# Three normed attentions of a two-stack transformer, written out pair by pair, with the next pair's queries and keys prepared during a pair's softmax

## The chip, the cores and the metric

The kernel runs on one core of one Trainium2 chip, as one launch. The metric is the device time of that launch in microseconds. The core has TensorE (PE), VectorE (DVE), ScalarE (ACT), GpSimd (POOL, unused here) and the queue of SyncE (SP), which issues the loads of weights. The engines run side by side and wait for each other on semaphores.

## The reference

A sequence of 256 tokens with 1024 features, all in float32, goes through two stacks of layers.

- Two layers of the first stack: `h = h + mix(norm(h)) @ w_out`, a gated feed-forward part and a gated projection of a side input. The mix concatenates a differential attention ("da": 4 heads, each with two query and key parts of 64 features and values of 128), a state-space mixer and a gated linear attention.
- Four layers of the second stack: a modulated norm, an attention, a gated add, another modulated norm and a feed-forward part. The attentions are, in order, stick-breaking ("sb"), block attention ("moba", here plain causal attention, since 256 tokens are one block), sliding window of 128 with sinks ("swa": 16 query heads, 2 key and value heads), and "sb" again.

In da, moba and swa (the three normed kinds) queries and keys are normed per head and turned by rotary angles:

```python
q = apply_rope(rms_norm(q, gain_q), cos, sin)
k = apply_rope(rms_norm(k, gain_k), cos, sin)
p = softmax(mask(q @ k.T / 8))          # da: softmax 1 - lambda * softmax 2
y = p @ v                               # da: rms_norm(y, g_sub) * (1 - lambda_init)
out = concat(y) @ w_out
```

## The kernel before

Activations are kept transposed: features on the 128 partitions, 256 tokens along the free dimension. A product with a weight is made in three fp32r matmuls (high part by high part, low activation by high weight, high activation by low weight, `three()`, L597 to L599), so each weight tile of 128x1024 is loaded by SP into a slot of `wslot`, rounded to `w_hi` by ACT (L1144, 1 us), and its rest `w_lo` made by DVE (L1506 or L1512, 1.2 us), which also frees the slot for SP's next load. Loads are issued by SP in a fixed order; for an attention it is, for each i: query tile i+1, key tile i+1, value tile i+1, output tile i, each when its slot is free.

An attention works on one pair of 64-wide heads at a time (one 128-wide tile; da: the two parts of one head). da has 4 such pairs and runs in two layers, moba 8, swa 8 in two groups of four. All pairs of a group in swa share one key and value tile, so a key and value tile is new ("fresh") for pairs 0 and 4 alone; in the others it is new for every pair. For a pair the work is:

- PE: project queries, and keys when fresh (24 matmuls each into `bank` 0); project values (L724, two halves of 16 recorded matmuls, plain fp32, into `bank` 1); sum squares over a head (L731); turn (L767); scores (L681, L682, into `bank` 2 and 3); transpose the weights of the softmax (L700, back into `bank` 2 and 3); values (L713, L714, `bank` 3, in da `bank` 1); da: sum squares of y (L735); output projection (24 matmuls into `acc`, L597 to L599).
- ACT: square (L1198), inverse root by Ln and Exp (L1148, L1150), exponentials of the softmax (L1242, L1247), copies of the transposed weights to `pt`, of the values to `v_sb` and of y to `y_hi` (all L1144), and the roundings of weight tiles.
- DVE: norming (L1487), the products with cos (L1614) and sin (L1616) and their sum (L1618, makes `qk`), mask and row maximum (L1487, L1630 to L1637), scaling by the inverse sum (L1537 to L1543), and the low parts of weight tiles and of y.

The order within a step of the loop, `whole(i, prior)`, is for PE: project queries and keys of pair i; transpose the weights of pair i-1; first half of the values of i; square sums of i; (moba, swa) y of pair i-1; second half of the values; (da) y of i-1; turn i; (moba, swa) output of i-1; scores of i; (da) output of i-1. So the softmax of pair i runs on DVE and ACT while PE is at the next step's projections of queries and keys. After the last pair there is nothing left to project: PE waits for its softmax, transposes, forms y and projects it. The middle steps run in a loop of the program (`Fori`), the first and the last are written out (`segments`).

## Time and profile before

| | us |
|---|---|
| median of 3 runs | 2418.82 (2411.75 to 2422.43) |
| profiled execution | 2425.04 |
| its span in the trace | 2423.1 |
| mean granted clock of TensorE | 0.959 |

Busy time of PE is 2239.9 us, of PE's weight loads 2101.7, of DVE 1576.0, of ACT 1073.9. The attentions that the change touches lie at these times of the trace: da of layer 0 from 28 to 130 us, da of layer 1 from 530 to 622, moba from 1379 to 1528, swa from 1745 to 1878. A step is read here from the start of one pair's scores to the start of the next pair's. The granted clock is 1.00 for 2.4 GHz and 0.50 for 1.2 GHz; a value between says which part of the stretch ran at either.

### The profile page before, as it was taken

What the parts mean: (1) busy time and instruction counts of PE and PEld (TensorE: products, weight loads), DVE (VectorE), ACT (ScalarE), POOL (GpSimd) and SP (SyncE); (2) the same over time, 40 slices, a digit from 0 to 9 for tenths busy, and PEclk for the clock granted to TensorE, in tenths of its full rate; (3) what the DMA queues carried; (4) which work ended last, traced back from release to release, by engine and by line L of the source; (5) the groups of instructions that cost most, each with busy time, mean ns of one, the idle gap of its engine ahead of it and who ended that gap; (6) DMA issues with size and microseconds to landing.
All of it is one profiled execution on the core that took longest, in us unless ns stands there. A gap on an engine that the chain in (4) does not pass through costs nothing.

```text
span 2423.1 us, 45499 instructions
## 1 busy us (share of the span) xinstructions
PE 2239.9 (92%) x17460; PEld 2101.7 (87%) x17460; DVE 1576.0 (65%) x2623; ACT 1073.9 (44%) x1728; POOL 0.2 (0%) x4
## 2 busy tenths in 40 slices
PE   5889999898889999899899999899987999998998
PEld 4788899877888999798899888799865999898998
DVE  4576677735665787366787866688866555666554
ACT  3445444324454443255444444444445444555442
POOL 0000000000000000000000000000000000000000
PEclk8999999998999999899999999899988999998999
DMA  4355399843552998454599654499832466442664
GB/s 135 89 148 156 114 302 291 257 126 106 140 143 82 300 298 276 133 156 132 163 300 299 217 155 142 138 297 300 250 88 87 130 186 187 139 138 86 192 182 138
DMA packets 549140, 436.19 MB, mean 180 GB/s; under 512 B 27664, under 2 KB 475192, under 8 KB 548920
## 3 DMA queue, kind: packets, MB, share of 16 engines
q1 hardware_dynamic: 545680, 431.22, 58.5%
q10 hardware_dynamic: 3368, 3.71, 0.5%
q8 instruction: 62, 1.02, 0.2%
q14 instruction: 30, 0.25, 0.0%
HBM read 433.82 MB, written 1.05 MB: 179 GB/s over the span
## 4 chain that ended last, share of the span: by engine, by line
PE 80%; DVE 10%; ACT 4%; DMA 2%; DVEq 2%; issue 2%; ACTq 1%; SPq 0%
PE bank L597 13%; PE bank L599 13%; PE bank L598 13%; PE acc L597 7%; PE acc L598 7%; PE acc L599 7%; PE bank L724 5%; PE bank L1111 2%; PE bank L1019 2%; ACT w_hi L1144 1%; PE bank L607 1%; DVE head_work L1487 1%; DVE w_lo L1512 1%; PE bank L767 1%; PE bank L713 1%
## 5 line engine op out<-in xcount | busy, mean ns | idle before, releaser
L597 PE MATMUL bank<-h_hi,w_hi 128*128 128x256 f32 x3024 | 856.7, 283 | 17.2 <-DVE w_lo L1512 4.6
L599 PE MATMUL bank<-h_hi,w_lo 128*128 128x256 f32 x3024 | 845.2, 279 | 0.0
L598 PE MATMUL bank<-h_lo,w_hi 128*128 128x256 f32 x3024 | 845.2, 279 | 0.0
L1144 ACT ACTIVATE w_hi<-wslot 128x1024 fp32r<-128x1024 f32 x574 | 595.2, 1055 | 516.7 <-PE acc L599 285.1
L1512 DVE TENSOR_TENSOR w_lo<-wslot,w_hi 128x1024 fp32r<-128x1024 f32 x396 | 474.5, 1221 | 229.8 <-ACT w_hi L1144 229.3
L597 PEld LDWEIGHTS bank<-h_hi,w_hi 128*128 128x128 f32 x3024 | 571.3, 189 | 41.2 <-issue 10.8
L599 PEld LDWEIGHTS bank<-h_hi,w_lo 128*128 128x128 f32 x3024 | 574.5, 190 | 0.0
L598 PEld LDWEIGHTS bank<-h_lo,w_hi 128*128 128x128 f32 x3024 | 572.2, 189 | 0.1
L597 PE MATMUL acc<-mid_hi,w_hi 128*128 128x256 f32 x1120 | 317.4, 283 | 5.2 <-DVE mid_lo L1803 3.2
L599 PE MATMUL acc<-mid_hi,w_lo 128*128 128x256 f32 x1120 | 312.6, 279 | 0.0
L598 PE MATMUL acc<-mid_lo,w_hi 128*128 128x256 f32 x1120 | 312.6, 279 | 0.0
L1487 DVE SCALAR_TENSOR_TENSOR head_work<-wslot,c_act,head_work 128x512 f32<-128x512 f32 x288 | 216.4, 751 | 24.0
L597 PEld LDWEIGHTS acc<-mid_hi,w_hi 128*128 128x128 f32 x1120 | 210.5, 188 | 7.5 <-DVE mid_lo L1803 3.6
L599 PEld LDWEIGHTS acc<-mid_hi,w_lo 128*128 128x128 f32 x1120 | 212.4, 190 | 0.0
L598 PEld LDWEIGHTS acc<-mid_lo,w_hi 128*128 128x128 f32 x1120 | 211.1, 188 | 0.0
L1506 DVE TENSOR_TENSOR w_lo<-wslot,w_hi 128x1024 fp32r<-128x1024 f32 x114 | 136.2, 1220 | 46.8 <-ACT w_hi L1144 46.6
L597 PE MATMUL acc<-y_hi,w_hi 128*128 128x256 f32 x384 | 128.2, 334 | 21.9 <-DVE y_lo L1556 21.9
L724 PEld LDWEIGHTS bank<-wslot,hT 128*128 128x128 f32 x1088 | 128.8, 193 | 9.1 <-issue 9.1
L724 PE MATMUL bank<-wslot,hT 128*128 128x128 f32 x1088 | 135.7, 279 | 0.0
L598 PE MATMUL acc<-y_lo,w_hi 128*128 128x256 f32 x384 | 119.2, 310 | 0.0
L599 PE MATMUL acc<-y_hi,w_lo 128*128 128x256 f32 x384 | 118.5, 309 | 0.0
L597 PEld LDWEIGHTS acc<-y_hi,w_hi 128*128 128x128 f32 x384 | 85.6, 223 | 30.5 <-issue 29.4
(267 smaller groups left out, 2497.8 us busy)
## 6 DMA issues: line engine op xcount, KB each, us to landing
wslot<-in_ada_w_dram SPq DMA_DIRECT2D x192, 512.0 KB, 5.8
wslot<-in_ffn_w_gate_dram SPq DMA_DIRECT2D x88, 512.0 KB, 4.8
wslot<-in_ffn_w_up_dram SPq DMA_DIRECT2D x88, 512.0 KB, 5.4
wslot<-in_ffn_w_down_dram SPq DMA_DIRECT2D x88, 512.0 KB, 3.5
wslot<-in_w_in_dram SPq DMA_DIRECT2D x72, 512.0 KB, 4.2
wslot<-in_sb_w_in_dram SPq DMA_DIRECT2D x48, 512.0 KB, 4.9
wslot<-in_w_ffn_gate_dram SPq DMA_DIRECT2D x44, 512.0 KB, 4.8
wslot<-in_w_ffn_up_dram SPq DMA_DIRECT2D x44, 512.0 KB, 5.5
```

Source lines behind the costliest of these rows:

```text
L597: pe.matmul(dst, w_hi[:, w, cols], hi, start=start, stop=False, skip_group_check=True)
L598: pe.matmul(dst, w_hi[:, w, cols], lo, start=False, stop=False, skip_group_check=True)
L599: return pe.matmul(dst, w_lo[:, w, cols], hi, start=False, stop=stop, skip_group_check=True)
L607: mm = pe.matmul(B(3, m, m + 1), ada_rows[:, P * m:P * m + P], C("ones", 0, 1), start=True, stop=True)
L713: pe.matmul(bank[c, y_bank, 0:256], v_sb[:, 0, c], pt[:, hh, 0:256], start=True, stop=False)
L724: mm = pe.matmul(B(1, 256 + P * t, 384 + P * t), hT[:, k, P * t:P * t + P], wk(2, k), start=(k == 0), stop=(k == KT - 1))
L1019: mm = pe.matmul(B(0, 0, 256), C("ones"), sqT[:, k, :], start=(k == 0), stop=(k == KT - 1))
L1111: mm = pe.matmul(B(2 * b, 0, 256), wk(s, k), xT[:, k, :], start=(k == 0), stop=(k == KT - 1))
L1144: return act.activation(dst, src, ACT.Copy)
L1487: return dve.scalar_tensor_tensor(out=out, in0=x, scalar=scalar, in1=y, op0=op0, op1=op1)
L1506: dve.tensor_tensor(w_lo[:, part, :], wslot[:, n, :], w_hi[:, part, :], ALU.subtract)\
L1512: dve.tensor_tensor(w_lo[:, part, :], wslot[:, n, :], w_hi[:, part, :], ALU.subtract).then_inc(slot_used[n], 1)
```

## The change

The function `attention` of each engine becomes two: `stick` for sb, which issues what it issued before (one wait that was long met is left out on PE), and `ahead` for da, moba and swa, which is written out for every pair, with no loop. SP's order is as it was. PE's order becomes:

```python
project(0); norm_sums(0); project_v(0); turn(0)
for i in range(n):
    more = i + 1 < n
    scores(i)
    if i and att == "da": out_sums(i - 1)
    if more: project(i + 1)
    whole = not more or fresh(i + 1)
    if i: out(i - 1, range(KT) if whole else range(4))
    if more:
        norm_sums(i + 1)
        if fresh(i + 1): project_v(i + 1)
    if i and not whole: out(i - 1, range(4, KT))
    if more: turn(i + 1)
    turn_weights(i)          # the transposes, L700 before
    values(i)
if att == "da": out_sums(n - 1)
out(n - 1, range(KT), att != "da")
```

ACT's order:

```python
square(0); root(0); v_copy(0); qk_high(1)
for i in range(n):
    if i and att == "da": y_root(i - 1)
    exps(i)
    if i and att == "da": y_high(i - 1)
    if more: square(i + 1)
    if i + 2 < n: qk_high(i + 2)          # else, not in da: two roundings for the feed-forward part
    if more: root(i + 1)
    if i: act.wait_ge(unit_done[3], g("unit_done3") + i)
    mix_high(3, PART_DOWN, unit_loads(at, att, 3, i))
    if more and fresh(i + 1): v_copy(i + 1)
    for hh in range(heads): ...           # copies of the transposed weights to pt
    act.wait_ge(sem["pv_done"], g("pv_done") + i + 1)
    ...                                   # da: square of y; else: y_hi
```

DVE's order:

```python
qk_normed(0); qk_turned(0); qk_low(1)
for i in range(n):
    maxima(i)
    if i and att == "da": y_normed(i - 1); y_low(i - 1)
    end_softmax(i)
    if i + 2 < n: qk_low(i + 2)           # else, not in da: two low parts for the feed-forward part
    if more: qk_normed(i + 1); qk_turned(i + 1)
    mix_low(3, PART_DOWN, i)
    if att != "da": y_low(i)
```

The tiles move in PSUM: square sums of queries and keys go from `bank` 2 to `bank` 1; values from `bank` 1 to columns 384 to 512 of `bank` 2 and 3; y of moba and swa from `bank` 3 to `bank` 1; the square sums of da's y to the second half of `bank` 1. `v_sb` is used in two halves in turn. New waits on PE: `project_v(i)` waits for the row maxima of pair i-1 (for pair 0 for a step of the modulation units that is older), the scores of pair 0 and the transposes ahead of a fresh pair wait for the copy of the values.

```diff
-                def whole(i, prior, kv, fresh, new_kv, more):
-                    ...
-                    proj_qk(i, ki, fresh, prior is None)
-                    if prior is not None:
-                        middle(prior)
-                    ...
-                    scores(i)
-                    if att == "da" and prior is not None:
-                        out(prior)
+                def project_v(i):
+
+                    loads = 32 if att == "swa" else 16
+                    pe.wait_ge(slot_full[2], 16 * (g("slot2") + g("extra2")) + loads * (group(i) + 1))
+                    pe.wait_ge(sem["h_ready"], g("h_ready"))
+                    if i:
+                        pe.wait_ge(sem["negmax"], g("negmax") + 2 * i)
+                    elif g("ada_stored"):
+                        pe.wait_ge(sem["ada_stored"], g("ada_stored") - 1)
+                    for t in range(TT):
+                        for k in range(KT):
+                            mm = pe.matmul(B(2 + t, 384, 512), hT[:, k, P * t:P * t + P], wk(2, k), start=(k == 0), stop=(k == KT - 1))
+                    mm.then_inc(slot_used[2], 1)
+                def values(i):
+                    width = P // heads
+                    v = P * (group(i) % 2)
+                    pe.wait_ge(sem["v_copied"], g("v_copied") + group(i) + 1)
+                    pe.wait_ge(sem["pt_ready"], g("pt_ready") + heads * i + heads)
+                    for hh in range(heads):
+                        c, d = slice(width * hh, width * hh + width), slice(v + width * hh, v + width * hh + width)
+                        pe.matmul(bank[c, 1, 0:256], v_sb[:, 0, d], pt[:, hh, 0:256], start=True, stop=False)
+                        mm = pe.matmul(bank[c, 1, 128:256], v_sb[:, 1, d], pt[:, hh, 256:384], start=False, stop=True)
+                    mm.then_inc(sem["pv_done"], 1)
```

## Rows read from the trace of the kernel before

**Rows 1.** The page's first part: busy us, share of the span, instructions, by engine.

```profile
PE 2239.9 (92%) x17460; PEld 2101.7 (87%) x17460; DVE 1576.0 (65%) x2623; ACT 1073.9 (44%) x1728; POOL 0.2 (0%) x4
```

**Rows 2.** Windows from scores to scores: length, busy by engine, clock, DMA share, GB/s.

```profile
53.65:69.83 16.18, 13.80 (x101) 11.68 (x102) 10.49 (x23) 6.97 (x18) 0.00 (x0) 1.00 0.49 142
69.83:91.61 21.78, 17.89 (x126) 16.00 (x126) 11.47 (x25) 9.08 (x21) 0.00 (x0) 0.92 0.34 98
...
113.49:130.30 16.81, 11.66 (x64) 10.29 (x65) 8.23 (x20) 6.57 (x16) 0.00 (x0) 0.80 0.50 125
...
560.31:583.05 22.74, 18.85 (x126) 16.96 (x126) 11.47 (x25) 9.09 (x21) 0.00 (x0) 0.85 0.33 95
...
1395.85:1415.05 19.20, 19.20 (x130) 16.88 (x130) 11.47 (x24) 8.15 (x18) 0.00 (x0) 0.83 0.53 143
1431.26:1447.48 16.22, 16.22 (x132) 14.22 (x131) 10.41 (x23) 8.17 (x18) 0.00 (x0) 1.00 0.41 127
...
1512.36:1528.17 15.81, 9.30 (x49) 7.72 (x48) 7.46 (x17) 7.46 (x15) 0.00 (x0) 0.69 0.24 71
...
1804.47:1820.74 16.27, 16.27 (x131) 14.21 (x130) 10.03 (x25) 7.58 (x19) 0.00 (x0) 1.00 0.22 65
...
1834.76:1848.71 13.95, 11.24 (x75) 8.56 (x75) 8.50 (x22) 6.73 (x18) 0.00 (x0) 0.88 0.25 75
...
1862.75:1878.19 15.44, 8.43 (x50) 6.97 (x49) 7.29 (x19) 7.95 (x17) 0.00 (x0) 0.67 0.24 68
```

**Rows 3.** PE's timeline, one middle step of moba: start, duration, what.

```profile
1431.26 0.50 PE L681 MATMUL bank<-head_work 64*128 64x128 f32 x4
...
1437.69 0.82 PE L700 MATMUL bank<-const,pr 128*128 128x128 f32 x6
1438.34 1.95 PE L724 MATMUL bank<-wslot,hT 128*128 128x128 f32 x16
1440.13 1.02 PE L731 MATMUL bank<-head_work,const 128*128 128x512 f32 x2
...
1441.89 2.05 PE L724 MATMUL bank<-wslot,hT 128*128 128x128 f32 x16
1443.78 1.02 PE L767 MATMUL bank<-head_work,const 128*128 128x512 f32 x2
```

**Rows 4.** PE's timeline in a middle step of swa, scores at 1820.74.

```profile
1827.03 1.00 PE L700 MATMUL bank<-const,pr 128*128 128x128 f32 x6 [2.42 <-DVE pr L1543]
1828.23 0.69 PE L731 MATMUL bank<-head_work,const 128*128 128x256 f32 x2 [0.20 <-ACT pt L1144]
```

**Rows 5.** DVE's timeline in the same step of swa.

```profile
1821.70 0.56 DVE L1487 SCALAR_TENSOR_TENSOR sm<-bank,const 128x384 f32<-128x384 f32 x1 [0.92 <-PE bank L682]
...
1827.09 0.35 DVE L1543 TENSOR_SCALAR pr<-pr,rinv 128x256 f32<-128x256 f32 x1
1827.35 1.22 DVE L1506 TENSOR_TENSOR w_lo<-wslot,w_hi 128x1024 fp32r<-128x1024 f32 x1
```

**Rows 6.** ACT's timeline in the same step of swa.

```profile
1825.72 0.19 ACT L1247 ACTIVATION_READ_ACCUMULATOR pr<-sm,nmx 128x1 f32 x1
...
1827.61 0.95 ACT L1144 ACTIVATE pt<-bank 128x384 f32<-128x384 f32 x2 [0.50 <-PE bank L700]
1828.96 0.47 ACT L1148 ACTIVATE head_work<-bank,epst 128x256 f32<-128x256 f32 x1 [0.40 <-PE bank L731]
```

**Rows 7.** PE's timeline, last step of da in layer 0, whose scores start at 113.49.

```profile
120.41 0.55 PE L700 MATMUL bank<-const,pr 128*128 128x128 f32 x3 [0.92 <-DVE pr L1487]
...
121.58 0.67 PE L713 MATMUL bank<-pt,v_sb 128*128 128x256 f32 x2 [0.63 <-issue]
...
123.04 0.67 PE L735 MATMUL bank<-ysq,const 128*128 128x256 f32 x2 [0.56 <-ACT ysq L1213]
```

**Rows 8.** Landing of the loads into wslot (L441) in moba, 1415 to 1465 us.

```profile
DMA to landing us min/median/max: 3.6/4.2/5.0
```

**Rows 9.** Landing of swa's half-tile loads of keys and values (L459).

```profile
DMA to landing us min/median/max: 4.7/5.4/8.2
```

More of the change, by code:

```diff
@@ L780, in attention, with whole @@
-                for lo, hi, *seg in segments(att, ph["n"]):
-                    if hi - lo == 1:
-                        whole(lo, lo - 1 if lo else None, *seg)
-                    else:
-                        with pe.Fori(0, hi - lo) as j:
-                            whole(j + lo, j + (lo - 1), *seg)
-                last = n - 1
-                middle(last)
-                values(last, 1 if att == "swa" else last)
+                def whole(i, prior):
+                    project(i, prior is None)
+                    if prior is not None:
+                        later_sums(prior)
+                        pe.wait_ge(sem["v_copied"], g("v_copied") + i)
+                    project_v(i, 0)
+                    if prior is not None:
+                        values(prior)
+                    project_v(i, 1)
+                    if prior is not None:
+                        out(prior)
+                    scores(i)
@@ L1256, in attention @@
[L1256 to L1262 removed]
+                    mix_high(3, PART_DOWN, unit_loads(at, "sb", 3, i))
+                    if not more:
+                        high(0, 2, unit_loads(at, "sb", 0, n))
@@ new lines, in ahead, with qk_low @@
+                mix_low = lambda m, part, i: low_of(m, part, g(f"high{m}") + i + 1)
+                heads = 1 if att == "da" else 2
+                group, fresh = grouping(att, n)
+                gains = qk_gains(att, l)
+                cos, sin = (cos1[:, :], sin1[:, :]) if att == "da" else (C("cos2"), C("sin2"))
+                mask = C("window") if att == "swa" else C("causal")
+                def qk_low(i):
+                    mix_low(0, 0, i)
+                    if fresh(i):
+                        mix_low(1, 1, group(i))
@@ L1612, in whole, with qk_normed @@
+                def qk_normed(i):
+                    sides = 2 if fresh(i) else 1
+                    dve.wait_ge(sem["qk_rs"], g("qk_rs") + i + 1)
+                    for side in range(sides):
+                        c = slice(256 * side, 256 * side + 256)
+                        last = stt(qkn[:, c], bank[:, 0, c], gains[side], rs2[:, c])
+                    last.then_inc(sem["qk_n"], 1)
                     dve.drain()
                     each = lambda ap: ap.rearrange("p (a s) -> p a s", a=sides)
-                    dve.tensor_tensor(each(qkc[:, 0:width]), each(qkn[:, 0:width]), per_tile(cos, sides), ALU.mult)
+                    dve.tensor_tensor(each(qkc[:, 0:256 * sides]), each(qkn[:, 0:256 * sides]), per_tile(cos, sides), ALU.mult)
@@ L1615, in whole, with qk_turned @@
+                def qk_turned(i):
+                    sides = 2 if fresh(i) else 1
+                    width = 256 * sides
+                    each = lambda ap: ap.rearrange("p (a s) -> p a s", a=sides)
                     dve.wait_ge(sem["qk_rot"], g("qk_rot") + i + 1)
```

548 lines of the change are left out of this document (296 added, 252 removed).

## The prediction

> **What bounds the kernel now.** I read the page first: PE is busy for 2239.9 us of the span, 92% [rows 1], so time can come only from PE's idle stretches, from stretches at the lower clock, and from what PE is given to do. PE's work is not changed in amount. I then cut the attentions into windows from one pair's scores to the next pair's [rows 2]. Three pictures come out. A middle step of moba takes 16.22 us, PE is busy for all of it and the clock is 1.00: nothing can be won there. A middle step of da takes 21.78 us with PE busy for 17.9 at a clock of 0.92; the four such steps are 21.78, 21.88, 22.74 and 21.91 long. A step of swa whose next pair shares keys and values takes about 14 us (six of them, the row shown is 13.95, the longest 14.50) with PE busy for 11.2 at 0.88. Last I took the timelines of single steps for the order and the price of each piece [rows 3 to 7].
>
> **Prices of the pieces**, start to start at full clock [rows 3]: scores 0.86; a fresh projection of queries and keys 5.57 (1432.12 to 1437.69), of queries alone half, 2.78; six transposes 0.65; each half of the values' projection 1.79; square sums 0.95; turn 0.95; values' product 0.80; an output projection 2.75 (from 1443.78 plus the turn to the next scores at 1447.48). They add up to 16.2 for a fresh step. With one-sided sums and turn (0.5 each) and no values a swa step is 8.8, a fresh da step with its three transposes and one more square sum is about 16.3.
>
> **The chain beside PE**, counted from the start of the scores at 1820.74 [rows 4 to 6]: mask at +0.96, exponentials done at +5.2, scaled weights done at +6.7, first transpose at +6.3. From the square sums' matmul to Ln 0.73; Ln and Exp take 0.97 for one side, 1.3 for two. From the turn to the next scores it is 2.57 for two sides (1.06 to the product with sin, then three DVE steps).
>
> **The stall that the new order brings.** Transposes and the product that reads their copy now stand next to each other on PE. In the trace there lies other work between them. ACT's two copies start 0.58 after the first transpose and take 0.95 [rows 4, 6], so the product starts 1.6 after it, where PE was free after 0.65: 0.95 idle in each pair of moba and swa. For da it is one copy; the last step of layer 0 shows the pair next to each other already, from 120.41 to 121.58 = 1.17, of which PE idles 0.84 at full clock. The bounds are 0.6 (the idle stretch that the row itself gives) [rows 7] and 1.3. Queued behind the product on PE is the next pair's scores and so its whole softmax, so this is paid in full.
>
> **A middle step of moba.** Scores 0.86, projection to 6.43, output to 9.18, sums to 10.1, values' projection to 13.7, turn to 14.7, transposes, stall to 16.3, product to 17.1. The norm (root ends at 11.6, normed at 12.5) is in time, `qk` is ready at 13.7 + 2.6 = 16.3. So 17.1 against 16.22: 0.9 slower, six times: **+5.4**. The first step (19.20 before at a clock of 0.83) loses the output projection (2.75), which goes to the end, and gains the stall and 0.8 of waiting for the square: **-1.1**. In the last step (15.81, PE idle 6.5) the output of pair 6 fills part of the wait for the softmax. Transposes start at 5.8 as before; ACT has one rounding ahead of the copies and not two, so the output starts about 1 us sooner; with the clock still low: **-1.5**. Moba: **+2.8**.
>
> **A middle step of da.** 0.86 + 0.5 + 5.57 + 2.75 + 0.95 + 3.6 + 0.95 + 0.33 = 15.5, stall 0.84, product 0.76: 17.05. y of the pair before is normed on DVE after the maxima (+3.9), rounded by ACT after the exponentials (+4.9), its low part done at 5.8; PE wants it at 7.0. PE's waits of before, 3.9 us in all (21.78 less 17.89), for the root of y ahead of the scores and then for `y_lo`, are gone, and with them the drop of the clock. Against 21.78, 21.88, 22.74, 21.91 that is 4.7 + 4.8 + 5.7 + 4.9 = **-20.1**. The first steps: -1.6 in layer 0 (16.18 before) and 0 in layer 1. The head of layer 0 is **+1.8**: half of the values' projection was done while ACT was still making the rotary tables, and now all of it stands behind the sums. The last steps get worse: the output of pair 2 waits for `y_lo` until 5.8 with nothing to cover it, where it started right behind the scores; PE idles for 4.4, so it runs at half clock (5.1), and transposes start at 10.9 where they started at 6.9 (120.41 less 113.49). **+3.5** in each layer, bounds +1.7 (clock up) and +4. Da: -20.1 - 1.6 + 1.8 + 7 = **-12.9**.
>
> **A step of swa within a group.** PE is free of its projection at 3.6 and of four output tiles at 5.0; ACT's square waits for the exponentials (5.1), sums at 5.5 to 6.1, second half of the output to 7.4. ACT rounds q(i+2) (5.4 to 6.4), then the root, to 7.3. DVE ends the softmax at 6.7, makes the low part of q(i+2) (1.22) [rows 5], and norms at 7.8 to 8.2: PE turns at 8.3 after a wait of 0.85. Transposes 8.8, product 10.4, end 11.2. So **11.2**, idle 0.5 + 0.85 + 0.95, against about 14: 2.8 less. Steps 1 to 2, 4 to 5 and 5 to 6 give -3.3, -2.8, -2.75. Step 0 to 1 starts at the lower clock: -1.4. In step 2 to 3 the keys of the second group are wanted one step earlier, and their half tiles land late, 4.7 to 8.2 after issue, with slow issues [rows 9]: +3, so +0.1 in all. Step 3 to 4 is a fresh one: 17.1 against 16.27, +0.8. Step 6 to 7 carries two roundings for the feed-forward part: -1.6. The last, 15.44 before, -1.8. Swa: **-12.75**.
>
> **Costs taken as nothing.** Without the loops: two turns of moba's loop both take 16.22 with PE busy throughout [rows 2], so a turn costs nothing now. The heads of layer 1's da, moba and swa: square sums come sooner, but the values' projection (da) and DVE's work on the modulation units (moba, swa) set the turn as before. The earlier roundings: SP now issues output tile i and queries i+2 at the very start of step i, since the slot of output i-1 is freed only after the norming. At 3.6 to 5.0 to land [rows 8] queries are there at about 4.5 to 5.4, ACT wants them at 5.4 in swa and at 7.1 or later elsewhere; keys two issues later.
>
> The Trainium skill, in "Runtime: NRT & Kernel Launch", section "Instruction fetch mechanics", says that a taken branch can force a fetch of instructions by DMA and advises unrolling. If each of the nine loop turns that go had cost one landing of rows 8 (4.2), the kernel would gain 38 us more, by an estimate; the two equal turns of moba speak against it.
>
> **Sum.** +2.8 - 12.9 - 12.75 = **-22.9**. Against the profiled execution, 2425.04, that is 2402.1; the median of the runs shown is 6.2 lower, 2418.82, which gives **2396**.
>
> **Rivals.**
>
> 1. The clock falls in swa in spite of shorter stalls. For: 2.3 us of 11.2 are idle, in three pieces. Against: up to 123.04 in the last step of da PE idled in three pieces, 0.92, 0.63 and 0.56, and the sums at 123.04 still took 0.67, what the values' matmuls took before them [rows 7]; the falls in swa follow one idle stretch of 2.42 [rows 4]. Price: a step at 0.88 has a quarter of 13.95 at half clock, 1.7 us of lost work [rows 2]; six steps: +10. Total -13, **2406**. The Trainium skill, "TensorE: Matmul & The Clock Gate", section "A second HAM failure mode: psum-queue depth-cycling", tells of a kernel whose short pauses between groups of matmuls made the clock swing; by it this rival would be the forecast. Chance 0.15.
> 2. The copies overlap better than I think, or a gap is hidden. Without the copy stall (19 pairs, 17 us) it is -40: **2379**. Rows 7 show the stall, so 0.08.
> 3. On the other side: weights come late. SP's in-order queue holds queries i+2 behind output tile i, which waits for the end of DVE's step. ACT's rounding stands ahead of the root, the root ahead of turn, transposes and the next scores: each us beyond the slack is a us in 16 steps. The point is a landing 4.9 after issue in swa and about 9.5 in fresh steps. At 2.2 us past it in each, +35: **+12, 2431**. Against: 5.0 is the longest whole-tile landing [rows 8], and 41% of the DMA engines are in use in moba [rows 2]. Chance 0.12.
> 4. The gains of da and swa are mostly eaten by waits between engines that I have not placed (five in-order hand-overs in a swa step, each taken at 0.05 to 0.1): -10 to 0, **2413**. Chance 0.15.
>
> My forecast has 0.50. What a measurement of this kernel tells from no change is about 0.5%, 12.1 us. The forecast and rival 2 are beyond it, and half of rival 1: 0.66 faster. Half of rival 1 and rival 4: 0.22 the same. Rival 3: 0.12 slower. The range goes from near rival 2, 2378, to 2418, past rival 4 and short of rival 3.
>
> **What would show it.** Right: middle steps of da near 17.0 with a clock of 1.00, steps of swa near 11.2, of moba near 17.1 with an idle stretch of 0.95 ahead of the values' product released by ACT's copies; the last step of da longer than before, with PE waiting over 4 us for `y_lo`. Wrong: moba's steps still 16.2 (no copy stall); swa at 13 or more with a clock under 0.95 (rival 1); ACT idle on a load into slot 0, 1 or 3 (rival 3).

## The result

The changed kernel takes **2392.3 us** (median of 7 runs, 2383.0 to 2396.5) against 2417.3 for the kernel before on the same chip (2409.4 to 2422.4): ratio 0.9894, 95% interval 0.9876 to 0.9911. The forecast was 2396. In a later comparison on another occasion the same kernel gave 2393.5 and 0.9899 (0.9867 to 0.9931).

The profiled execution has a span of 2390.4 us. Its engine line answers to [rows 1]: PE is busy 24.0 us less, with the same 17460 instructions. Of this 12.6 lie in the three attentions, where the granted clock is higher (over swa 0.90, and 0.87 before); the other 11.4 lie in the other stages, in several of which one and the same matmul took 281 ns in the first profile and 276 in this one (more on this at the second profile of the kernel before, among the experiments).

```profile
PE 2215.9 (93%) x17460; PEld 2083.6 (87%) x17460; DVE 1579.9 (66%) x2623; ACT 1076.5 (45%) x1728; POOL 0.2 (0%) x4
```

The windows of the changed kernel, from one pair's scores to the next pair's, answer to [rows 2] (length, then busy time by engine, granted clock, DMA share, GB/s):

```profile
54.70:69.62 14.92, 13.36 (x99) 11.38 (x100) 11.86 (x24) 7.50 (x16) 0.00 (x0) 1.00 0.49 145
69.62:86.47 16.85, 16.18 (x127) 14.40 (x126) 11.45 (x25) 9.35 (x20) 0.00 (x0) 1.00 0.44 126
...
585.73:607.39 21.66, 13.12 (x69) 11.47 (x68) 9.08 (x21) 7.55 (x19) 0.00 (x0) 0.76 0.82 201
1373.97:1391.16 17.19, 15.47 (x107) 12.97 (x107) 11.99 (x23) 7.87 (x17) 0.00 (x0) 0.90 0.65 177
1408.24:1425.33 17.09, 16.36 (x133) 14.57 (x131) 10.65 (x23) 8.37 (x18) 0.00 (x0) 1.00 0.45 123
...
1743.21:1755.98 12.77, 9.16 (x50) 6.80 (x50) 9.14 (x22) 6.27 (x17) 0.00 (x0) 0.77 0.15 42
1768.05:1782.69 14.64, 10.14 (x76) 8.41 (x75) 9.74 (x23) 7.72 (x19) 0.00 (x0) 0.92 0.63 144
1782.69:1801.61 18.92, 18.20 (x132) 16.08 (x130) 9.42 (x23) 7.80 (x19) 0.00 (x0) 0.88 0.18 57
1801.61:1813.05 11.44, 9.51 (x76) 8.17 (x74) 8.96 (x23) 6.71 (x18) 0.00 (x0) 1.00 0.33 92
```

A middle step of da takes 16.85 at a clock of 1.00, where it took 21.78 at 0.92. Moba's is 17.09, with PE busy for all but 0.73, against 16.22. A swa step within a group takes 11.44 to 12.07, the last one before the end of swa 13.44. Besides moba's, two kinds of window are worse than before: da's last step (21.66, clock 0.76) and the fourth step of swa (18.92, clock 0.88), with the late-key step ahead of it (14.64).

To see where the 32.7 us between the two spans went, I divided both traces at the matmuls of the norm on either side of each attention; in da the far mark is the first matmul of the mixer's small projection. The last two columns are a second profile of each kernel, taken with the experiments below.

| stretch | before | changed | difference | second profiles |
|---|---|---|---|---|
| da, layer 0 | 109.7 | 105.6 | -4.1 | 111.3, 105.9 |
| da, layer 1 | 101.8 | 94.0 | -7.8 | 104.1, 92.9 |
| moba | 160.6 | 162.4 | +1.8 | 157.8, 161.2 |
| swa | 144.1 | 136.8 | -7.3 | 145.5, 139.1 |
| the four | 516.1 | 498.8 | -17.4 | 518.7, 499.1 |
| all the rest | 1907.0 | 1891.6 | -15.4 | 1898.2, 1893.6 |

So the attentions give 17 to 20 us by both pairs of profiles. The rest of the difference lies in the other stages. Their only edit is the wait left out of the stick-breaking attention, whose middle steps take 15.65 to 15.84 before and after.

In a middle step of moba PE's timeline shows the new order, and its one gap (start, duration, what, in brackets the idle time before it and what ended it), answering to [rows 3]:

```profile
1422.12 1.02 PE L771 MATMUL bank<-head_work,const 128*128 128x512 f32 x2
1422.98 0.82 PE L791 MATMUL bank<-const,pr 128*128 128x128 f32 x6
1424.52 0.66 PE L801 MATMUL bank<-pt,v_sb 128*64 128x256 f32 x4 [0.72 <-ACT pt L1196]
1424.97 0.42 PE L802 MATMUL bank<-pt,v_sb 128*64 128x128 f32 x4
1425.33 0.50 PE L780 MATMUL bank<-head_work 64*128 64x128 f32 x4
```

Turn, transposes, the bare copy (0.72), values' product, scores: as forecast, with a gap of 0.72 in place of 0.95.

In swa the late keys show as the longest wait of PE. These are its timeline around the fourth pair's turn, and the turns of the sixth and the seventh pair, which have no new keys behind them:

```profile
1779.13 0.70 PE L771 MATMUL bank<-head_work,const 128*128 128x256 f32 x2 [3.51 <-DVE head_work L1583]
1779.66 0.82 PE L791 MATMUL bank<-const,pr 128*128 128x128 f32 x6
1781.21 1.13 PE L801 MATMUL bank<-pt,v_sb 128*64 128x256 f32 x4 [0.72 <-ACT pt L1196]
...
1810.17 0.70 PE L771 MATMUL bank<-head_work,const 128*128 128x256 f32 x2 [0.96 <-DVE head_work L1583]
...
1822.07 0.70 PE L771 MATMUL bank<-head_work,const 128*128 128x256 f32 x2 [1.45 <-DVE head_work L1583]
```

The wait of 3.51 is followed by half clock: the product at 1781.21 takes 1.13, not 0.66. DVE's norm is named as the releaser of all three turns, but ACT's timeline ahead of the last of them shows what was late, and DVE's how it reaches the norm:

```profile
1819.31 1.06 ACT L1196 ACTIVATE w_hi<-wslot 128x1024 fp32r<-128x1024 f32 x1 [0.81 <-DMA wslot<-in_swa_w_in_dram]
1820.27 0.46 ACT L1200 ACTIVATE head_work<-bank,epst 128x256 f32<-128x256 f32 x1
1820.80 0.42 ACT L1202 ACTIVATE head_work<-head_work 128x256 f32<-128x256 f32 x1
```

```profile
1820.40 1.22 DVE L1602 TENSOR_TENSOR w_lo<-wslot,w_hi 128x1024 fp32r<-128x1024 f32 x1 [0.64 <-ACT w_hi L1196]
1821.54 0.48 DVE L1583 SCALAR_TENSOR_TENSOR head_work<-bank,pcol,head_work 128x256 f32<-128x256 f32 x1
```

The rounding of the weights of the pair after next waits for their landing. Two things that the norm needs stand behind it: the root in ACT's order, done at 1821.22, and the low part of the same weights in DVE's order, done at about 1821.6. The second ends last here, by some 0.3 to 0.4.

### The profile page after: what moved, and what is told of

Read it like the earlier page. It is cut to its first block, busy times and chain, and to the rows that moved or that the text cites. A ratio compares the mean times of both kernels' runs of the same rounds, so it can differ in the third digit from the quotient of the medians.

```text
span 2390.4 us, 45059 instructions
## 1 busy us (share of the span) xinstructions
PE 2215.9 (93%) x17460; PEld 2083.6 (87%) x17460; DVE 1579.9 (66%) x2623; ACT 1076.5 (45%) x1728; POOL 0.2 (0%) x4
## 4 chain that ended last, share of the span: by engine, by line
PE 79%; DVE 9%; ACT 5%; DMA 4%; DVEq 1%; issue 1%; ACTq 1%; SPq 0%
PE bank L604 13%; PE bank L606 13%; PE bank L605 13%; PE acc L604 7%; PE acc L606 6%; PE acc L605 6%; PE bank L707 3%; PE bank L1163 2%; PE bank L1071 2%; PE bank L760 2%; ACT w_hi L1196 2%; DVE w_lo L1608 1%; PE bank L614 1%; DVE head_work L1583 1%; DMA wslot<-in_swa_w_in_dram 1%
## 5 line engine op out<-in xcount | busy, mean ns | idle before, releaser
L604 PEld LDWEIGHTS bank<-h_hi,w_hi 128*128 128x128 f32 x3024 | 571.1, 189 | 40.8 <-issue 11.1
L1602 DVE TENSOR_TENSOR w_lo<-wslot,w_hi 128x1024 fp32r<-128x1024 f32 x114 | 136.8, 1221 | 77.2 <-ACT w_hi L1196 77.0
L604 PE MATMUL acc<-y_hi,w_hi 128*128 128x256 f32 x384 | 121.4, 316 | 18.5 <-DVE y_lo L1745 15.8
L1552 ACT ACTIVATE silu_g<-bank 128x256 f32<-128x256 f32 x132 | 49.5, 375 | 115.8 <-PE bank L606 115.4
L2133 DVE TENSOR_TENSOR mid<-silu_g,bank 128x256 f32<-128x256 f32 x132 | 55.1, 417 | 61.3 <-ACT silu_g L1552 61.1
```

The costliest lines, as they stand in the source:

```text
L604: pe.matmul(dst, w_hi[:, w, cols], hi, start=start, stop=False, skip_group_check=True)
L1552: act.activation(silu_g[:, b, :], B(b, 0, 256), ACT.Silu).then_inc(sem["silu_ready"], 1)
L1602: dve.tensor_tensor(w_lo[:, part, :], wslot[:, n, :], w_hi[:, part, :], ALU.subtract)\
L2133: dve.tensor_tensor(mid[:, b, :], silu_g[:, b, :], B(b, 256, 512), ALU.mult).then_inc(sem["mid"], 1)
```

## The experiments

Each stretch below is measured between the same marks as in the table. The times of whole kernels scatter by some 10 us from run to run, so where 1 to 5 us are in question the steps of the profile decide.

**Moba alone in the old order.** The old function is kept beside the new one and called for moba:

```
-                    (stick if ph["att"] == "sb" else ahead)(ph, at)
+                    (stick if ph["att"] == "sb" else attention_old if ph["att"] in ('moba',) else ahead)(ph, at)
```

> The changed kernel with the moba attention alone as it was before the change (its three-part order, its loop over the middle pairs, values' bank as it was); da and swa as changed. Theory: the changed order costs moba 0.87 us a pair, 0.72 of it the bare copy behind the transposes, so here the steps of moba go back to 16.2 (first 19.2) from 17.09 (first 17.19), the stretch between the norms on its two sides from 162.4 to about 160.6, and the time is about 2 us below that of the changed kernel (ratio to before near 0.989). Rival: the longer step comes from something that reaches the whole kernel (the longer straight instruction stream, other addresses); then the steps stay near 17.1 and nothing is won. In both cases the steps of da stay at 16.85 and those of swa at 11.4 to 18.9.

Measured: 2396.5 us, ratio 0.9916 (0.9892 to 0.9941). The middle steps of moba are back at 16.20 to 16.23 (the first step is 17.79, not the 19.2 expected); its stretch is 158.6. Da's middle steps stay at 16.86 and 17.15. So the longer step comes with the new order, as the theory says, but not all of the 0.87 is the order's own price. Moba's middle steps in the new order take 16.79 or 17.09 in the nine profiles that have it as it stands in the changed kernel (38 steps and 16), and the 0.30 between the two is the level of the same matmul, 276 or 281 ns, as set out at the second profile of the kernel before. The 24 middle steps in the old order, in four profiles, all ran at the faster level. At equal level the order costs 0.57 a step. In the whole time it does not show: the interval holds the changed kernel's ratio too.

**Transposes early in da and moba**, so that the copy is covered:

```
                     whole = not more or fresh(i + 1)
+                    if early: turn_weights(i)      # PE; ACT copies behind the square
                     ...
-                    turn_weights(i)
                     values(i)
```

> In da and moba the transposes of a pair's weights stand right behind the projection of the next pair instead of behind the turn, and ScalarE copies them then; the output of the pair before and the values' projection run while it copies. swa is as changed. Theory: the copy is what TensorE waits for in each middle step (0.67 in da, 0.72 in moba), and both are gone: da's middle steps fall from 16.85 to about 16.2, moba's from 17.09 to about 16.4, all together 2 x 3 x 0.65 + 7 x 0.7 = 8.8 us less (time near 2383). Rival A: the wait only moves, to the transposes, which now wait for the softmax (weights ready 6.2 to 7.3 after the scores, the projection done at 6.8): up to 0.5 in da, near nothing in moba; then da stays at 16.7 and the total is 5 to 6. Rival B: ScalarE's roundings of the next weights come 1.4 later and VectorE's behind them, and the turn waits instead: steps stay where they are.

Measured: 2398.4 us, ratio 0.9921 (0.9899 to 0.9944). Da's middle steps are 17.50 to 17.52, moba's 16.81 to 17.11. None of the three texts gave the size in da, whose steps got 0.66 longer; the mechanism of rival A, transposes that wait for the softmax, is part of it. PE's timeline of a middle step of moba, and DVE's behind the same turn:

```profile
1431.48 1.02 PE L773 MATMUL bank<-head_work,const 128*128 128x512 f32 x2
1432.44 0.66 PE L803 MATMUL bank<-pt,v_sb 128*64 128x256 f32 x4
1432.92 0.40 PE L804 MATMUL bank<-pt,v_sb 128*64 128x128 f32 x4
1434.06 0.50 PE L782 MATMUL bank<-head_work 64*128 64x128 f32 x4 [0.74 <-DVE head_work L1711]
```

```profile
1432.55 0.69 DVE L1709 TENSOR_TENSOR head_work<-bank,const 128x512 f32<-128x512 f32 x1 [1.35 <-PE bank L773]
1433.31 0.69 DVE L1711 TENSOR_TENSOR head_work<-head_work 128x512 f32<-128x512 f32 x1
```

The copy's 0.72 is gone and 0.74 stands ahead of the scores. From the turn to the next scores it is 2.58 by way of DVE (the product with sin and the sum), and 3.21 by way of transposes, copy and product in the changed kernel. The copy stall had lain beside this chain; taking it away bares the chain and could give 0.63 at most. In moba the six transposes themselves, 0.57, now stand ahead of the turn instead of filling time behind it, so next to nothing is left. In da the gain behind the turn is 0.27 (2.84 to 2.57), and ahead of it 0.94 is added: the weights of the softmax are ready 7.4 after the scores, where the output had started at 6.85 (0.54, which includes a wait of 0.18 to 0.37), the transposes take 0.30, and the output ran at the slower of two levels (0.10). The level of the projection does not matter there: with the faster one the wait for the weights is longer by as much, and the step is 17.50 all the same.

**The second keys and values asked for early** (SP's order in swa):

```
-                            for n in range(3) if new_kv else (0,):
+                            for n in range(3) if new_kv and not grouped else (0,):
                             ...
+                            if lo == 0 and grouped:
+                                for n in (1, 2): kv_load(w, n, 1, u[n] + 2)
```

> The four loads of swa's second group of keys and values are asked for in the first pair instead of in the fourth; all else as changed. Theory: in the step before the second group the turn waits 3.5 us because the keys land late, and the idle time drops the clock for the first 7 us of the next step. With the keys there, that step falls from 14.6 to about 12.1 and the next one from 18.9 to about 17.1 (projection 5.9 in place of 7.1, scores and values at full clock), 4 to 4.5 us in all. Rival A: the wait is VectorE's and ScalarE's work for two weight tiles more, not the transfer: then the turn still waits 2 us or more, the clock still falls, and less than 1.5 us is won. Rival B: the wait goes but the clock falls all the same, since all steps of swa leave TensorE idle: 14.6 to 12.1, and 18.9 stays: 2.5 us.

Measured: 2397.2 us, ratio 0.9918 (0.9891 to 0.9944). The windows of the third to fourth and of the fourth to fifth pair:

```profile
1769.33:1782.30 12.97, 10.31 (x76) 8.56 (x74) 9.55 (x23) 7.60 (x19) 0.00 (x0) 0.92 0.26 82
1782.30:1801.57 19.27, 18.55 (x133) 16.43 (x131) 9.42 (x23) 7.79 (x19) 0.00 (x0) 0.87 0.19 56
```

The late-key step falls from 14.64 to 12.97; the wait before the turn is 1.82 instead of 3.51. The step behind it stays at half clock for its projection, though the wait that precedes it is shorter: rival B. Late keys cost 1.7 us; the clock is a matter of its own. The length of a wait alone does not foretell it: in this run one wait of 1.82 ahead of a turn (at 1778.74) is followed by half clock from 1780.3, and another of 1.82 (at 1833.68) by full clock until 1845. And swa's stretch is 136.6, no shorter than before the edit. The first step takes 14.0 in place of 12.8, and the last pair, up to the norm, 18.5 in place of 16.6. In the first step ACT's timeline shows the rounding waiting for the next queries; in the changed kernel it waited for nothing there:

```profile
1750.11 1.06 ACT L1199 ACTIVATE w_hi<-wslot 128x1024 fp32r<-128x1024 f32 x1 [1.19 <-DMA wslot<-in_swa_w_in_dram]
1751.07 0.46 ACT L1203 ACTIVATE head_work<-bank,epst 128x256 f32<-128x256 f32 x1
```

In SP's queue the four loads now stand ahead of two for the feed-forward part and of these queries. The two are issued at 1741.2 and 1742.0, some 20 us later than in the changed kernel; the queries themselves are issued 1.59 after the scores against 1.29. How much of the wait of 1.19 comes from the transfers in front of them is not shown.

**The tail of da.** In the last pair y goes ahead of the second head's softmax:

```
                 maxima:   after head 0, if da and last pair:  y_normed(i - 1); y_low(i - 1)
                 ACT:      y_high(i - 1) ahead of exps(i); pt's copy ahead of w_hi's rounding
```

> In the last pair of da alone: VectorE norms and rounds the y of the pair before between the maxima of the two heads, ScalarE rounds that y ahead of the exponentials, and copies the transposed weights ahead of the rounding of the output weights. Theory: the output of the pair before waits for y's low part (4.21 us), which waits in line behind the softmax; here it starts 1.5 earlier, and the copy no longer waits 1.05 behind the rounding: the last steps of da (21.66 and about the same in layer 0) fall to about 19.7, 4 us in all. Rival A: the softmax, now 1.3 later, is what the transposes wait for (weights ready 8.6 after the scores against an output that ends at 9.3), and half or less is left, 0 to 1 a layer. Rival B: with a shorter idle time the clock holds and the output takes 3.0 instead of 5.1: then about 17.5 a step and 8 us in all.

Measured: 2389.9 us, ratio 0.9876 (0.9845 to 0.9908). The last steps are 18.86 and 19.43 where they were 22.37 and 21.66, 5.7 us in all. First the changed kernel's timeline in layer 1, then this one's:

```profile
591.50 0.55 PE L604 MATMUL acc<-y_hi,w_hi 128*128 128x256 f32 x1 [4.21 <-DVE y_lo L1745]
...
596.46 0.49 PE L791 MATMUL bank<-const,pr 128*128 128x128 f32 x3
598.24 0.67 PE L801 MATMUL bank<-pt,v_sb 128*128 128x256 f32 x2 [1.29 <-ACT pt L1196]
...
602.87 0.55 PE L604 MATMUL acc<-y_hi,w_hi 128*128 128x256 f32 x1 [2.57 <-DVE y_lo L1745]
```

```profile
589.69 0.36 PE L604 MATMUL acc<-y_hi,w_hi 128*128 128x256 f32 x1 [2.57 <-DVE y_lo L1755]
...
593.81 0.55 PE L791 MATMUL bank<-const,pr 128*128 128x128 f32 x3 [1.14 <-DVE pr L1590]
595.03 0.67 PE L801 MATMUL bank<-pt,v_sb 128*128 128x256 f32 x2 [0.67 <-ACT pt L1196]
...
599.65 0.55 PE L604 MATMUL acc<-y_hi,w_hi 128*128 128x256 f32 x1 [2.57 <-DVE y_lo L1755]
```

The wait for `y_lo` fell from 4.21 to 2.57, and in layer 1 the first output then ran at full clock (its first matmul takes 0.36, not 0.55). In layer 0 the same wait of 2.57 was followed by half clock, and the output took 4.43 where it took about 3.0 in layer 1. In layer 1 the softmax became the later one (1.14). Theory and both rivals each hold a part.

**The kernel before, profiled again.**

> The kernel before, unchanged, for a second profile of it. The two profiles compared so far differ by 32.7 us in span, but only 17.7 of that lie in the three attentions; the rest is in feed-forward stages that no edit touches, where a three-pass matmul takes 281 ns in one profile and 276 in the other. Theory: those two levels come and go from run to run of one and the same program, so this profile shows the same steps in the attentions (21.8 in da, 16.2 in moba, 14.0 in swa, within 0.3) and other lengths of the feed-forward stages (anywhere from 197 to 204 for the last). Rival: the level belongs to the program, as its instruction stream is laid out; then the feed-forward stages repeat to a tenth of a us (252.9, 252.1, 204.9, 205.7, 203.8), and some 15 us of the gain are the change's, by that way.

Measured: 2426.7 us in 8 runs, ratio to the same kernel's other runs 1.0024 (0.9998 to 1.0050), which shows how far chance alone can move a ratio. The span is 2416.9, where the first profile had 2423.1. Its middle steps repeat (da 21.8, 21.7, 22.5, 21.6; moba 16.22; swa 13.9 to 14.4) but its other stages do not, and neither do da's last steps, up to the mixer's projection: 18.7 in both layers against 17.05, since the output of the last pair took 5.3 at half clock where it had taken 4.26, and the sums ahead of it ran at half clock too. This is the row of one of the three products in the last feed-forward stage, first in the first profile of before, then in the second:

```profile
L598 PE MATMUL bank<-h_lo,w_hi 128*128 128x256 f32 x352 | 98.9, 281 | 0.0
```

```profile
L598 PE MATMUL bank<-h_lo,w_hi 128*128 128x256 f32 x352 | 97.2, 276 | 0.0
```

Same program, same instructions, 281 ns or 276: this stage is 203.9 long in the one and 197.2 in the other. The rival falls. Nor does the length go with the edits: it is 203.9 in four of the twelve profiles of the changed kernel and its variants as well, and 197.3 to 198.0 in the other eight.

**Swa: VectorE turns first, then makes the low part.**

```
+                    if att == "swa" and more: qk_normed(i + 1); qk_turned(i + 1)
                     if i + 2 < n: qk_low(i + 2)
```

> In swa alone VectorE norms and turns the next pair's queries before it makes the low part of the weights of the pair after that, not behind it. Theory: in the steps with no new keys the turn waits 0.2 to 1.8 us for the norm, which stands in line behind that rounding (1.22 us); with it gone those steps fall from 11.4 to 12.1 to about 10.6 to 11, four steps, 3 to 4 us, and the spell of half clock behind the longest wait (1.82) goes with it, 1.3 more. Rival A: VectorE's work is only moved: the rounding now stands ahead of y's low part and of the next pair's maxima, and the softmax of the next pair starts later by what was won; then the steps stay within 0.3. Rival B: with less idle time the transposes wait for nothing but the copy's 0.72, which stays: a step of 10.2.

Measured: 2406.7 us, ratio 0.9938 (0.9914 to 0.9962), nothing won and something lost: the interval lies above that of the changed kernel (0.9876 to 0.9911). The swa steps are 10.8, 13.7, 14.8, 19.0, 12.6, 14.8, 12.4; the stretch is 140.2. Neither theory had the cause, which is in ACT's timeline:

```profile
1820.77 1.06 ACT L1196 ACTIVATE w_hi<-wslot 128x1024 fp32r<-128x1024 f32 x1 [1.83 <-DMA wslot<-in_swa_w_in_dram]
1821.74 0.46 ACT L1200 ACTIVATE head_work<-bank,epst 128x256 f32<-128x256 f32 x1
```

A low part is what frees a weight slot. Moved behind the turn, the queries' low part pushes the output tile's back as well, and SP, which issues in order, asks for the next queries 2.10 after the scores of this step (at 1815.21), where the changed kernel does so after 0.97. The rounding waits 1.83 for the landing, and the root behind the rounding makes the turn wait 2.14.

**The waits filled** with matmuls that nobody reads:

```
+                    if att == "swa" and more and not fresh(i + 1):
+                        fill(B(3, 384, 512), {0: 10, 2: 12}.get(i, 6))
                     if more: turn(i + 1)
```

> The changed kernel with matmuls added whose results nobody reads, in the places where TensorE waits in swa (10 of 128 columns ahead of the first turn, 12 ahead of the third, 6 ahead of the others with no new keys; 2 of 256 columns behind the transposes) and in the last pair of each of the three attentions (da: 11 ahead of the output of the pair before, 3, 1 and 7 in the waits behind it). Theory: idle time of 1.8 us and more is followed by half clock (da's output of the pair before takes 5.1 in place of 2.9, swa's steps lose 1.3 to 2.5 in three places); with the waits filled the granted clock stays at 1.0 there. The last steps of da fall from 22.4 and 21.7 to about 18.3 (output 2.1 less, last output 1.6 less), swa's stretch by 4 to 6, all together 10 to 13 us: time near 2381. Rival A: the clock falls all the same in swa, as even a filled wait of f32 matmuls with 128 columns doesn't hold it: da gains, swa stays. Rival B: the added matmuls run longer than the waits that they fill, and each step pays 0.1 to 0.5 for them: nothing is left in swa.

Measured: 2383.2 us, ratio 0.9846 (0.9798 to 0.9895). Its windows of most of swa and of da's last step in layer 1:

```profile
1736.50:1840.00 103.50, 98.55 (x747) 85.44 (x748) 70.84 (x176) 56.78 (x146) 0.00 (x0) 0.98 0.37 103
587.40:605.86 18.46, 18.42 (x113) 15.97 (x112) 9.11 (x21) 7.57 (x19) 0.00 (x0) 1.00 0.87 210
```

Da's last steps fall to 18.4 each, as the theory gives, with every wait still there: 3.9 and 3.2 us of them were the clock. Swa's clock goes to 0.98, its fourth step to 17.16 (18.92 before), its stretch to 133.9: 3 to 5 us less, somewhat under the theory. The late keys' step stays (14.98). Over the four stretches this is 489.3 us against 498.8 and 499.1, 9.5 less. The whole time does not settle it by itself, since the interval of four runs overlaps that of the changed kernel.

**Swa alone in the old order**, as the first experiment did for moba.

> The changed kernel with the swa attention alone as it was before the change. Theory: the changed order is worth 7.5 us between swa's first scores and the norm behind it (119.3 before, 111.8 after), not the 12.8 forecast; so here the steps go back to 13.9 to 14.5, 16.3 for the fourth and fifth pair, and the time is 7 us above that of the changed kernel (near 2399). Rival: part of swa's shorter steps is the run's own level (matmuls of 276 against 281 ns); then the old order in this program takes 117 or less and the change is worth under 5.

Measured: 2408.9 us, ratio 0.9941 (0.9915 to 0.9967). Stretch 143.5; steps 13.9, 13.1, 13.1, 16.5, 14.1, 14.2, 15.0. Against the changed kernel's 136.8 and 139.1 the new order is worth 4.4 to 6.8 us in this program; the theory said 7.5, and part of the rival holds. By the ratios the kernel is 10 to 11 us slower than the changed one; what goes beyond the stretch lies in the other stages (1903.8 against 1891.6 and 1893.6). Da alone was not put back to the old order. Its gain is read from its middle steps, 16.85 to 17.16 in all eleven profiles that have da's new order as it stands in the changed kernel, and 21.55 to 22.74 in the two of the kernel before.

**Everything that won, with the old and with the new moba.**

> The parts that won, together: da and swa in the changed order, moba in the order before; y ahead of the second head's softmax in the last pair of da; swa's second keys asked for in the first pair; added matmuls, whose results nobody reads, in the waits of swa and of the three last pairs (in da 7, 3, 2, 1 and 7). Theory: from the changed kernel's 2392, da's last steps give 2 x 4.5 (to 17.2), swa about 4 (133), moba's middle steps 0.57 to 0.87 each, 4 to 5: 2375, ratio 0.982. Rival: waits filled and waits shortened are the same time won once; then it is no better than the filled waits alone (ratio 0.985).

> As the run before this one, but moba in the changed order. Theory: moba's stretch is 3.5 to 5 us longer than with the old order (six steps of 17.1 or 16.8 against 16.22), the rest the same: ratio about 0.9835. Rival: the last pair gives it back, since the old order leaves TensorE 4.9 idle there and the new one less: both kernels the same within 1 us.

Measured: 2378.4 us, ratio 0.9834 (0.9805 to 0.9863) with the old moba, 2380.8, 0.9830 (0.9799 to 0.9862) with the new. Both beat the changed kernel, whose interval from the same comparison begins at 0.9867, but by the whole time neither can be told from the filled waits alone, which was the rival of the first expectation. By the four stretches they can: 481.8 and 480.2 against 489.3. Windows of the first of them, da's last step and the step of swa with new keys:

```profile
586.12:603.49 17.37, 17.33 (x108) 15.15 (x108) 9.27 (x21) 7.63 (x19) 0.00 (x0) 1.00 0.81 202
1772.11:1788.95 16.84, 16.84 (x137) 14.81 (x135) 9.40 (x23) 7.80 (x19) 0.00 (x0) 1.00 0.20 63
```

Da's last steps are 17.37, the late-key step 12.37, swa's stretch 132.0 (130.5 in the second). Moba's stretch is 155.9 with the old order and 159.0 with the new, but 1.7 of this difference lies ahead of the first scores. From the first scores to the norm it is 132.6 and 134.0: the middle steps cost 4.3, and the first step gives 2.8 back. This is not seen in the whole time.

**Swa: the root ahead of the rounding, and the turn ahead of the low part.**

```
                     square(i + 1)
+                    if att == "swa": root(i + 1)
                     if i + 2 < n: qk_high(i + 2)
```

> In swa alone ScalarE takes the inverse root of the next pair's sums ahead of the rounding of the weights of the pair after that, and VectorE norms and turns the queries ahead of their low part. Theory: what makes the turn late in swa is neither engine's work but a transfer: the rounding waits 0.35 to 1.8 us for the weights to land, and the root stands in line behind it. With both out of the line the turn waits for nothing (under 0.3), and the steps with no new keys fall from 11.4-12.1 to about 10.6-11, swa's stretch from 136.8 to about 132. Rival A: the slot is now freed about 2 us later, the next weights land that much later, and the projection waits for their low part instead: steps of 11.5 to 14, as when VectorE's order alone was changed (10.8, 13.7, 12.6, 14.8). Rival B: the root alone was late, and VectorE's order costs the same 1.2 elsewhere: steps of 11.4 to 12.1 as now.

Measured: 2391.0 us in 2 runs, ratio 0.9883 (0.9832 to 0.9934), too wide to tell from the changed kernel. Swa's steps are 10.9, 11.1, 13.6, 19.0, 12.1, 11.3, 11.7, the stretch is 133.3. One of its steps:

```profile
1812.36 0.70 PE L771 MATMUL bank<-head_work,const 128*128 128x256 f32 x2 [0.20 <-DVE head_work L1585]
1812.90 0.82 PE L791 MATMUL bank<-const,pr 128*128 128x128 f32 x6
1814.88 0.66 PE L801 MATMUL bank<-pt,v_sb 128*64 128x256 f32 x4 [1.16 <-ACT pt L1196]
```

The turn waits 0.16 to 0.20 for the norm in all steps up to the last turn, save the first (1.57) and the one that makes new keys, where it waits for nothing: with both the root and the norm out of the line behind the rounding, its wait for the transfer no longer reaches the turn. The root alone was not moved, so the two shares are not told apart. Rival A did not come. But the roundings now stand ahead of the copies of the transposed weights, and the product waits 0.87 to 1.81 instead of 0.72, and 2.81 in the late-key step: about half of the win is paid back there.

**The changed kernel again.**

> The changed kernel once more, for its own scatter and as the base of the other runs of this chip. Theory: steps of da at 16.85, moba at 17.1 or 16.8 (the two levels of the matmuls), last steps between 20.8 and 22.4, swa's stretch 136 to 137; feed-forward stages at either level; ratio 0.987 to 0.992. Rival: the 32.7 us between the two first profiles were the change's: then this profile's span is 2390 again against 2417 and 2423 of before, and the ratio stays at 0.989 or below.

Measured: 2393.5 us, ratio 0.9899 (0.9867 to 0.9931), span 2392.7. As the theory has it, except two of da's middle steps, which ran at the slower level and took 17.15, and swa, whose late-key step took 16.2 and whose stretch was 139.1. It tells nothing against the rival by itself; the second profile of before does.

## Why the prediction was right, and which terms were off

Time and direction were right, but that the time fits within 4 us is in part luck. The attentions gave 17.4 us where the sum has 22.9, and 15.4 us that nobody forecast lay in the other stages between the two profiles. By the attentions alone the time would have been about 2401, still within the range.

- **Middle steps of da**: 17.05 forecast (the terms as written add up to 17.1), 16.85 measured, 17.15 at the slower level of the matmul; -20.9 in place of -20.1. Right in mechanism and size, the clock of 1.00 too: the waits for the root of y and for `y_lo` are gone, and the copy's wait alone is left (0.67, for 0.84 forecast). This term alone is nearly the whole forecast of -22.9.
- **Head and first steps of da**: +1.8 in layer 0, measured +1.80. First steps -1.3 and -1.7 against -1.6 and 0.
- **Last steps of da**: +3.5 each with bounds +1.7 and +4; measured +5.3 and +4.6 by the first pair of profiles, outside the bounds, and +3.7 and +3.3 by the second, inside them. The place was right: `y_lo` at 5.8, output at half clock, transposes at 11.0 and 10.7. One thing behind it was not counted: ACT rounds the output weights (1.06) ahead of the copy as soon as the output is done, so the product waits 1.12 and 1.29, where 0.67 is the bare copy. The last output runs at half clock for the most part too (4.9 and 4.5), but so it did before (4.3 in one profile, 5.3 in the other), and this scatter is what parts the two pairs.
- **Moba**: +2.8 forecast, +1.8 measured (+3.3 by the second profiles). The step of 17.1 is met by luck: the stall is 0.72, not 0.95, and the 72 matmuls of the step happened to run at the slower level in this profile, which adds 0.30 and was in no term. At the faster level the step is 16.79. The first step gave 2.0, not 1.1, and the last pair 1.3 for 1.5. The old order gave 16.22 again inside the changed program, which shows that the rest is the order's. What I had not seen is that the stall is no loss that can be had back: 2.58 of the 3.21 between turn and scores is DVE's chain.
- **Swa**: -12.8 forecast, -7.3 measured. Here "a step of swa within a group: 11.2" was nearly met where ACT's rounding waited only 0.35 for its load (11.44); the one at 11.9 has ACT's rounding wait 0.81 for its load, with the root and DVE's low part behind it. The one at 12.07 starts at half clock, behind a wait of 2.10 for the first turn in which no rounding waits for a load. "Step 3 to 4: +0.8" was +2.65, since it starts at half clock. The late keys were +0.5 in place of +0.1.
- **The rivals.** The first, a falling clock in swa, came true in part: in the steps there are three spells of half clock, from 1753.2, 1780.5 and 1835.1, each about 7 us long, besides one of 3.4 us as the first scores start. Each of the three began within 1.4 us of the end of a wait of 1.8 to 3.5, ahead of the copy's 0.7, and none behind the short waits: the fifth step with waits of 0.25, 0.96 and 0.72 has a clock of 1.00. But waits of 1.82 and 2.57 were followed by full clock elsewhere (in the runs with the early keys and with the new tail), so what sets the fall stays open. Filling the waits gave the clock back (0.98). From the first scores of swa to the norm the clock even rose, from 0.86 to 0.89. The Trainium skill, "TensorE: Matmul & The Clock Gate", section "A second HAM failure mode: psum-queue depth-cycling", tells of a kernel in which frequent tiny pauses between groups of matmuls made the clock swing. The trace agrees in that swings cost time here (the fourth step took 18.92, and 17.16 with the waits filled); it shows them behind waits of 1.8 to 3.5 us, not behind tiny ones. The second rival is refuted by the 0.67 and 0.72 that stand ahead of each product. The third, weights late, cost PE something in swa alone, with waits of the rounding of 0.35 to 1.3 where they came, far under its price (moba's roundings wait 0.27 to 0.40 in two of its middle steps, which are 17.09 like the others). The mechanism described, a root in line behind a rounding that waits for its load, is half of it: DVE's low part behind the same rounding ended last. The fourth has no row of its own.
- **Not in the sum**: 5 to 15 us in the other stages. The two first profiles happened to have the feed-forward stages at different levels of the matmul. In the medians 25 us were found, in the attentions 17 to 20; whether the 5 to 8 between them are chance or something of the program's layout stays open. Twelve profiles of the changed kernel and its variants give 1891 to 1906 for all but the attentions, the two of before 1898 and 1907: they overlap.

## What to carry to other kernels

When work is reordered so that an engine waits less, write down what frees each buffer in the new order: a low part made 1.2 us later to please a chain delayed by 1.1 us the load that the same chain waited for a step later. A stall on the path is worth only its distance to the next chain beside it, less what the work moved to cover it costs in its new place; here 0.72 of copy was worth at most 0.63, and in practice nothing. Look at the last step of a loop as a case of its own: without the next pair's work to cover them, the waits made da's last steps 3.3 to 5.3 us longer, and filling them gave 3.2 to 3.9 back. And compare two profiles of one program before a difference between two programs is explained.

## What the hardware showed unexpectedly

- One and the same matmul (128x256, one of the three products of a projection) takes 276 ns in some stages and 281 in others, and the level changes between runs of one program: the last feed-forward stage takes 197 or 204 us, one before it 189 or 195, moba's middle step 16.79 or 17.09, in three of the profiles in turn from step to step. The granted clock does not tell the two apart: both kinds of moba step show 1.00, both lengths of the last stage 0.99. I have not found what sets it. It is a large part of the scatter between profiles here.
- Matmuls that nobody reads, put into waits of 0.7 to 4 us, made the four stretches 9.5 us shorter (489.3 against 498.8; the medians are 2383.2 and 2392.3), though each wait stayed as long as it was. Idle time cost twice here, once as such and once as half clock (1.2 GHz) for the work behind it: 3.9 and 3.2 us in da's last steps. Part of that the kernel before paid too, whose last output took 4.3 to 5.3 where the filled kernel's takes 3.0.
- A wait did not fix what came behind it: 2.57 us ahead of the output in da's last step was followed by half clock in layer 0 and by full clock in layer 1 of one and the same run.
